# One encoder layer on one core: conditioning parts moved to the first stage, residual loop reordered, affinities kept on chip, experts started on half the rows

## The reference, cut to what matters

```
mod = silu(c) @ w_ada + b_ada          # c: (1024), w_ada: (1024, 6*1024); 6 parts
sh1, sc1, ga1, sh2, sc2, ga2 = split(mod, 6)
h  = rms_norm(x, g_pre1) * (1 + sc1) + sh1
u  = h @ w_in                          # heads' columns, then two gate groups za, zb
y_ret, y_hg = retention(...), hgrn2(...)
merged = sigmoid(za) * (y_ret @ w_br_ret) + sigmoid(zb) * (y_hg @ w_br_hg)
x  = x + ga1 * rms_norm(merged @ w_out, g_post1)
h2 = rms_norm(x, g_pre2) * (1 + sc2) + sh2
aff = softmax(h2 @ w_router); gate, idx = top_k(aff.T, cap)   # 16 experts
x  = x + ga2 * rms_norm(experts(h2[idx]) * gate scattered back, g_post2)
```

## Time and profile before

| what | us |
|---|---|
| median of 3 runs (lowest, highest) | 2854.24 (2853.39, 2854.70) |
| the profiled execution's own time | 2856.68 |
| its span | 2854.7 |
| PE, DVE, ACT, POOL busy | 2665.3, 1786.0, 1335.4, 301.6 |

### The profile page before, as it was taken

One profiled execution on the slowest core, in us unless ns is written; L12 is line 12 of the kernel. 1 busy time (PEld: TensorE's weight loads), 2 busy tenths in 40 slices (PEclk: granted clock), 3 DMA queues, 4 the chain that ended last, 5 costly groups with the idle time before them and its releaser, 6 DMA issues. The chain is left out here.

```text
span 2854.7 us, 48423 instructions
## 1 busy us (share of the span) xinstructions
PE 2665.3 (93%) x20566; PEld 2132.8 (75%) x20566; DVE 1786.0 (63%) x2147; ACT 1335.4 (47%) x1410; POOL 301.6 (11%) x246
## 2 busy tenths in 40 slices
PE   5999999999999988983999999999999999999993
PEld 3788888889877877862777777777777777777772
DVE  4675757767400054547777777776777777777775
ACT  5544435354211121441555555555555555555552
POOL 2010000101000011211011101110111101110110
PEclk9999999999999999995999999999999999999996
DMA  7111011011343265236788788788888888887886
GB/s 283 33 31 44 24 35 55 23 52 31 115 158 126 72 209 166 97 105 242 276 286 298 286 300 289 276 295 291 294 289 296 295 289 284 282 300 286 284 290 230
DMA packets 285775, 564.97 MB, mean 198 GB/s; under 512 B 24680, under 2 KB 91080, under 8 KB 285304
## 3 DMA queue, kind: packets, MB, share of 16 engines
q1 hardware_dynamic: 274536, 540.79, 53.2%
q0 software_dynamic: 7680, 20.98, 3.2%
q10 hardware_dynamic: 3344, 0.11, 0.1%
HBM read 514.52 MB, written 47.28 MB: 197 GB/s over the span
## 5 line engine op out<-in xcount | busy, mean ns | idle before, releaser
L2291 DVE TENSOR_TENSOR we_low<-ring,we_high 128x2048 fp32r<-128x2048 f32 x384 | 878.1, 2291 | 366.5 <-ACT we_high L2240 366.5
L2240 ACT ACTIVATE we_high<-ring 128x2048 fp32r<-128x2048 f32 x384 | 737.4, 1922 | 438.9 <-PE ps_ey L2212 279.7
L1297 PE MATMUL ps_a<-h_high,w_high 128*128 128x512 f32 (+1 forms) x696 | 252.7, 363 | 7.7 <-ACT pair L817 4.8
L1298 PE MATMUL ps_a<-h_low,w_high 128*128 128x512 f32 (+1 forms) x696 | 247.6, 356 | 0.0
L1299 PE MATMUL ps_a<-h_high,w_low 128*128 128x512 f32 (+1 forms) x696 | 247.4, 356 | 0.0
L2179 PE MATMUL ps_ep<-ring,xp 128*32 128x256 f32 x4096 | 234.3, 381 | 0.0
L2210 PE MATMUL ps_ey<-we_high,hidT_high 128*128 128x512 f32 x512 | 206.6, 403 | 0.0
L2154 PE MATMUL ps_eg<-we_high,xs_high 128*128 128x512 f32 x512 | 206.2, 403 | 0.3 <-DVE xs_low L2315 0.3
L2179 PEld LDWEIGHTS ps_ep<-ring,xp 128*32 128x32 f32 x4096 | 126.6, 110 | 99.5 <-issue 22.5
L2156 PE MATMUL ps_eu<-we_high,xs_high 128*128 128x512 f32 x512 | 200.3, 391 | 0.0
L2157 PE MATMUL ps_eu<-we_low,xs_high 128*128 128x512 f32 x512 | 200.2, 391 | 0.0
(11 more groups left out here) (308 smaller groups left out, 4976.3 us busy)
## 6 DMA issues: line engine op xcount, KB each, us to landing
ring<-in_w_gate SPq DMA_DIRECT2D x256, 512.0 KB, 9.4
ring<-in_w_up SPq DMA_DIRECT2D x256, 512.0 KB, 10.5
ring<-in_w_down SPq DMA_DIRECT2D x256, 512.0 KB, 4.4
w_raw<-in_w_in SPq DMA_DIRECT2D x52, 512.0 KB, 3.8
w_ring<-in_w_ada SPq DMA_DIRECT2D x12, 1024.0 KB, 11.1
sig_dram<-sig SPq DMA_DIRECT2D x15, 640.0 KB, 7.1
w_ada_z<-in_w_ada SPq DMA_DIRECT2D x16, 512.0 KB, 6.9
sig_g<-sig_dram SPq DMA_DIRECT2D x16, 512.0 KB, 3.8
```

The lines of the kernel that those rows point to most:

```text
L1297: pe.matmul(out, w_high, x_high, start=start, stop=False)
L1298: pe.matmul(out, w_high, x_low, start=False, stop=False)
L2240: act.activation(w_high[:, s % SPLIT], t.ring[:, s % RAW], ACT.Copy).then_inc(s_high, 1)
L2291: dve.tensor_tensor(w_low[:, s % SPLIT], t.ring[:, s % RAW], w_high[:, s % SPLIT], ALU.subtract).then_inc(s_low, 1)
```

## The change: what it does, and the diff

Parts 3 and 4 of `w_ada` (8 pieces of 1 MiB) and `g_pre2` (1024 numbers as a column) are handled in the first stage, and the gates stage has none of it. The order of the first stage's transfers changes; the squares of the last two pairs of tiles, and their norms, move into the loop over tiles. In the residual stage norms and transposes come one iteration earlier, on ACT and DVE ahead of the newer tile; the last tile's x is added on DVE. The affinities go from SBUF to SBUF at the end of the residual stage. The experts' first products wait for one half of the rows, and PE's `turn_x(0, 2)` comes after the first two pieces.

```diff
-        PARTS = 3
+        PARTS = 5
+            load_w(0)
+            load_w(1)
             load_x(0)
-            load_w(0)
+            load_w(2)
+            load_w(3)
             load_x(1)
-            load_w(1)
+            load_w(4)
             load_x(2)
-            load_w(2)
+            load_w(5)
+            load_head(0)
+            load_w(6)
+            load_w(7)
             load_x(3)
-            load_w(3)
+            load_w(8)
             load_x(4)
-            load_head(0)
-            for j in range(4, NJ):
+            for j in range(9, 4 * PER):
                 load_w(j)
...
             load_head(1)
+            for j in range(4 * PER, NJ):
+                load_w(j)
             load_head(2)
...
                 if i == 0 and v >= 2:
-                    pe.wait_ge(s_modsb, v - 1)
+                    pe.wait_ge(s_modsb, max(v, 2))
...
-                if 2 <= tl < 2 + PER:
-                    mod_rows(COLS1 + tl - 2)
-                if tl in (6, 7):
-                    project(0, KC // 2 * (tl - 6), KC // 2 * (tl - 5))
-            project(1, 0, KC)
+                if tl >= 3:
+                    mod_rows(COLS1 + tl - 3)
+                if tl in (6, 8):
+                    project(0, KC // 4 * (tl - 6), KC // 4 * (tl - 4))
+            mod_rows(4 * PER - 1)
+            project(1, 0, KC // 2)
+            mod_rows(4 * PER)
+            project(1, KC // 2, KC)
+            mod_rows(4 * PER + 1)
             project(2, 0, KC)
+            mod_rows(4 * PER + 2)
+            mod_rows(4 * PER + 3)
+            pe.wait_ge(s_modsb, PARTS)
+            pe.wait_ge(s_xact, NT)
+            pe.wait_ge(s_xdve, NT)
+            columns((3, 4))
...
-                act.dma_start(pre_cols[:], t.g_pre1[0].rearrange("(c p) -> p c", p=P)).then_inc(s_small, 16)
+                for n, v in enumerate((t.g_pre1, t.g_pre2)):
+                    act.dma_start(pre_cols[:, n], v[0].rearrange("(c p) -> p c", p=P)).then_inc(s_small, 16)
...
-            for i in range(NX):
+            for i in range(3):
                 squares(i)
...
+                if tl in (1, 3):
+                    squares(3 + tl // 2)
+                if tl in (3, 5):
+                    root(3 + tl // 4)
...
-                if tl == 8:
+                if tl == 2:
+                    variance(3)
+                if tl == 4:
+                    norm(3)
+                    variance(4)
+                if tl == 6:
+                    norm(4)
+                if tl == 7:
                     rows(2)
                     gate_row(2)
...
+            rows(3)
             low(NT - 1)
+            rows(4)
+            scale_shift(1, t.scale2[:], t.shift2[:])
...
-                    if 3 <= k < 3 + KC and b != 1:
-                        ada(2 * (k - 3) + b // 2)
-                    if k == KC + 4 and b == 0:
-                        columns()
...
-            sp.dma_start(t.aff_dram, affT[:]).then_inc(s["st"], 16)
+            for r, (o, m) in enumerate(((SEQS[0], HALF), (SEQS[0] + HALF, HALF), (0, SEQS[0]))):
+                sp.dma_start(t.shared[r * NE:(r + 1) * NE, 0:m], affT[:, o:o + m]).then_inc(s["st"], 16)
...
-            for k in range(NT + 3):
+            for k in range(NT + 2):
                 if k < NT:
                     out(k)
-                if 2 <= k < NT + 2:
-                    turn(k - 2)
-                if k >= 3:
-                    route(k - 3)
+                if 1 <= k < NT + 1:
+                    turn(k - 1)
+                if k >= 2:
+                    route(k - 2)
...
-            for k in range(NT + 2):
+            for k in range(NT + 1):
+                if k >= 1:
+                    norm(k - 1)
                 if k < NT:
                     act.drain()
                     squares(k)
                 if k + 2 < NT:
                     high(k + 2)
-                if 1 <= k < NT + 1:
-                    norm(k - 1)
-                if k >= 2:
-                    modulate(k - 2)
+                if k >= 1:
+                    modulate(k - 1)
...
+                if tl == NT - 1:
+                    dve.wait_ge(s_x[tl % 3], 16 * (tl // 3 + 1))
+                    dve.wait_ge(s["x1"], tl)
+                    dve.tensor_tensor(x1[:, tl % 3], x1[:, tl % 3], x[:, tl % 3], ALU.add).then_inc(s["x1"], 1)
...
-                if i == 0:
-                    pe.wait_ge(s_xl, 2 * (e + 1))
-                    if b >= 1:
-                        pe.wait_ge(s_hid, b)
+                if i % 2 == 0:
+                    pe.wait_ge(s_xl, 2 * e + i // 2 + 1)
+                if i == 0 and b >= 1:
+                    pe.wait_ge(s_hid, b)
...
-            for r in range(3):
-                turn_x(0, r)
+            turn_x(0, 0)
+            turn_x(0, 1)
             for b in range(NBLK + 1):
                 if b < NBLK:
                     gate_up(b, 0)
                     gate_up(b, 1)
+                if b == 0:
+                    turn_x(0, 2)
```

More of the change, by code:

```diff
@@ L246, in _ @@
             pe.wait_ge(s_modsb, 2)
-            columns()
+            columns((0, 1))
             def project(b, c0, c1):
@@ L304, in _ @@
                     root(i - 1)
-            root(NX - 1)
+            root(2)
             act.wait_ge(s_first, 16)
@@ L338, in rows, with scale_shift @@
                 dve.wait_ge(s_mod, PER * (v + 1))
-                dve.tensor_tensor(mod[:, v], ps_mod[v % 2][:, 0:QW], bias[:, v], ALU.add).then_inc(s_modsb, 1)
-            def scale_shift(scale, shift):
-                dve.wait_ge(s_col, 1)
+                dve.tensor_tensor(mod[:, v], ps_mod[v][:, 0:QW], bias[:, v], ALU.add).then_inc(s_modsb, 1)
+            def scale_shift(n, scale, shift):
+                dve.wait_ge(s_col, n + 1)
                 for r in range(2):
@@ L355, in gate_row, with variance @@
                 dve.tensor_tensor(post[:], mod[:, v], post[:], ALU.mult).then_inc(s_rows, 1)
-            def norm(i):
+            def variance(i):
                 v = ssum[:, 2 * i:2 * i + 2]
@@ L376, in _ @@
             head_columns()
-            for i in range(NX):
+            for i in range(3):
+                variance(i)
                 norm(i)
@@ L1356, in _ @@
                 sp.dma_start(t.yT[:, m], t.yT_dram[m].rearrange("h p n -> p h n")).then_inc(t.s_branch, 16)
-            sp.wait_ge(s_zero, 1)
-            for r in range(2):
-                sp.dma_start(bias[r:P:32], t.b_ada[0][3 * D:5 * D].rearrange("(v g x) -> g v x", g=4, x=QW)).then_inc(s_vec, 16)
-            with nc.allow_non_contiguous_dma(reason="a vector into columns, once"):
-                sp.dma_start(pre_cols[:], t.g_pre2[0].rearrange("(c p) -> p c", p=P)).then_inc(s_vec, 16)
-            load_a(0)
-            load_a(1)
-            for s in t.head_sems:
-                sp.sem_clear(s)
             for k in range(1, NG):
@@ L1659, in _ @@
             pool.memset(zero[:], 0.0).then_inc(s["zero"], 1)
-            for tl in range(NT):
+            for tl in range(NT - 1):
                 pool.wait_ge(s["scaled"], tl + 1)
@@ L1830, in _ @@
             split(1)
-            for k in range(NT + 3):
+            for k in range(NT + 2):
+                if 1 <= k < NT + 1:
+                    variance(1, k - 1)
                 if k < NT:
@@ L1837, in _ @@
                 if 1 <= k < NT + 1:
-                    variance(1, k - 1)
-                if 2 <= k < NT + 2:
-                    modulate(k - 2)
-                if k >= 3:
-                    logits(k - 3)
+                    modulate(k - 1)
+                if k >= 2:
+                    logits(k - 2)
             dve.wait_ge(s["lt"], 1)
```

114 lines of the change are left out of this document (24 added, 90 removed).

## The result

| | before | changed |
|---|---|---|
| median us (lowest, highest) | 2853.53 (2850.98, 2857.42), 8 runs | 2863.1 (2861.89, 2864.38), 8 runs |
| span of the profiled execution | 2854.7 | 2861.1 |

The ratio is 1.0033, 95% interval [1.0024, 1.0042]: 9.6 us slower by the medians. The forecast was 2862.8 (2850 to 2869). The total fits, with luck: the step (a) of the first stage failed, and the terms of the gates stage and of the first stage were each too large by about 3 us or more, with opposite signs.

What follows compares the result with a forecast made beforehand. PE was taken as busy nearly throughout, so what counts is when it gets its work. The terms -17.2 + 22.5 + 1.3 - 0.7 + 2.7 sum to +8.6, giving 2862.8 us on the median's scale, range 2850 to 2869.

Steps and rivals of the forecast that it cites:

- gates stage: Steps 3 to 12 lose all work of the two w_ada parts, which nothing hides behind PE: -17.2 us.
- residual stage: Idle at the start 1.5, one more turn and route +2.9, tail -3.3, slow clock +0.4: about +1.3 us.
- (a): First stage: g_pre2's 1024 small packets cost 8.5 us (bounds 0 and 10.1), so DVE starts at 33.2 instead of 24.7.
- experts' start: First product earlier, but low(2) is late behind x_rows(0, 2), PE idles 3.3 us and its clock falls: +2.7 us.
- two waits for a transfer with the clock that they cost: Gates stage: part of the 17.2 us excess, 3.6 in step 5 (18.99 against 15.36) and another 0.85.
- third rival: The small packets fit in, costing about 1 us: first stage +15, total +1.1, 2855.3 us; chance 0.16.
- (b): First stage, DVE's start to first evacuation: at 51.5, 4.1 us later than now; the earlier weights bring nothing.
- (c): First stage, loop over tiles: piece 12 waits 3.8 us for rows(2), and the stage ends at 102.7 against 79.5.
- fourth rival: PE at the slow clock through the first stage: +30.5 there, total +16.6, 2870.8 us; chance 0.14.
- Transfers alone: Rival: only transfers set the first stage, ending at 82.5, so +3; total -10.9, 2843.3 us; chance 0.12.
- Half rows pay: Rival: if low(2) isn't late, the experts' start gains 2.9 us; total +3.0, 2857.2 us; chance 0.13.
- Slow clock: Rival: first stage near its upper bound from PE's gaps, +30.5; total +16.6, 2870.8 us; chance 0.14.

Runs made afterwards that it cites:

- f_silu_first: Changed kernel with ScalarE's c_silu and c_pad computed ahead of its issues for gn, bias and post: 2867.39 us, ratio 1.0048.
- e_small_alone: Kernel before with only g_pre2's column load added to ScalarE's queue behind g_pre1's (loaded, not used): 2860.68 us, ratio 1.0024.
- g_rows_early: a_low_first with VectorE's rows(2) and gate_row(2) moved ahead of tile 7's evacuation in the first stage: 2849.93 us, ratio 0.9985.
- b_experts_before: Changed kernel with the experts' start put back (three transposes first, both halves of the rows awaited): 2860.33 us, ratio 1.0021.
- a_low_first: Changed kernel with VectorE's low(2) and low(3) ahead of x_rows(0, 2) at the experts' start: 2857.3 us, ratio 1.0009.
- j_norm_early: g_rows_early with ScalarE's root(3) ahead of squares(4) and VectorE's norm(3) behind tile 3 instead of tile 4: 2851.3 us, ratio 0.9987.
- k_all: j_norm_early plus g_pre2's column issued late by SyncE, and the residual stage's old order with last addition on VectorE: 2847.93 us, ratio 0.9979.

## Why the prediction was right

The total was right by luck in part: two errors of opposite sign, each of some 3 us or more, cancel. Step by step, with what the runs put in its place:

| step | predicted | traces of the pair | other runs |
|---|---|---|---|
| gates stage | -17.2 | -17.6 | -13.1 to -14.1 |
| first stage | +22.5 | +19.8 | +17.4 to +19.5 |
| residual stage | +1.3 | +1.8 | +1.4 |
| affinities | -0.7 | -0.35 | -0.1 to -0.4 |
| experts' start | +2.7 | +3.4 | +3.4 by the ratios, +2.6 by the trace |

The first stage of the other runs: 99.26, 99.52 and 99.80 with the parts moved, 80.29 and 81.88 without. Taken back one at a time, the parts give 5.1 (both stages of the move), 3.4 and 2.3 us by the ratios; with the affinities that is 10.4 where 9.6 was measured, each of these figures being good to 3 us or so.

**Gates stage.** The mechanism holds, and the size holds for the two traces. The term "two waits for a transfer with the clock that they cost" (3.6 and 0.85) is the one that was mis-sized: they belong to one execution and not to the kernel. The profiled execution was 2.4 above the median in the table; I took these 2.4 off the sum instead of asking which term they sat in. The 17.2 already took the waits away, so part of the excess was taken off twice. On the median's scale the move gives 13.1 to 14.1 here, and with my other terms as they were the forecast would have been 2865.9 to 2866.9. That it came out within 0.3 us of the measured time is luck: the first stage's term was too large by about as much.

**First stage, (a).** This step failed as an account of the changed kernel: "DVE then starts at 33.2", and it starts at 24.8. Its price was real (6.75 alone, 7.4 in f_silu_first), but I priced the added load against the stream of before. The change rewrote that stream too: in SyncE's new order the fifth piece has to wait for PE by 6.3 us, and PE waited for ScalarE, whose issues the added packets held up. I had the rule that every queue a load stands in counts, and did not apply it to ScalarE's own instructions behind its issues. What I named as the third rival ("the small packets fit in") is what the trace shows, by another mechanism than its own. That equal counts speak against blocks of 9 to 17 was said too soon (e_small_alone, above).

**(b).** With (a) gone, the first evacuation is set by the weights and rows(1) (44.20); "the earlier weights bring nothing" was wrong by 3.2 us.

**(c).** The loop was predicted in the right places (3.8 us at piece 12, measured 3.79) but 4.4 us too short: from the transposes of tile 6 to the end 33.0 against 37.4. The difference is mostly PE at the slow clock behind its gaps (granted 0.57 from 60 to 68 us, so mostly at 1.2 of 2.4 GHz), which I had put into the upper bound and the fourth rival. That bound itself was summed too low: 7 pieces, 4 turns and 4 half blocks at 1.0, 1.0 and 2.75 us are 22 us of work, so at half speed they would add 22 and not 8. In sum the chain was 8.4 earlier than forecast at lb_diff and 7.4 at tile 6's transposes, and lost 4.4 of that behind them: 3.0 earlier than my walk's end of 102.7, 2.7 less than the term of 22.5. g_rows_early shows that the wait at piece 12 with its clock was worth 5.1 in the stage.

**Residual stage.** Its terms (1.5, 2.9, -3.3, 0.4) add up to 1.5 and not 1.3, and the steps to the norm to 12.3 and not 12.7. The two stalls (0.98 and 0.33; 1.0 and 0.5 predicted) and the idle 5.7 are as predicted. From the first to the last squares it is 3.8 more (4.4 predicted), and the tail gives back 2.0 (2.9 predicted), so the size is right with two small errors. Order and last addition together were taken back for 1.4. Of the last addition I had taken for granted that shorter is earlier; in the old order it is not.

**Affinities.** Three issues take 1.89 and not 1.2, and what follows them takes 2.7 and not 3.0, so half of the forecast's gain is left in this trace and less in two others.

**Experts' start.** Right in its mechanism, with the wait at 3.31 where 3.3 was forecast; b_experts_before and a_low_first confirm it from both sides.

**The rivals.** "Transfers alone" falls: piece 12 does wait for DVE, and g_rows_early still ends at 94. (PE's work behind the last tile's turn, put at 16.2 against it, is 16.6 by the walk's own times.) "Slow clock" was half there. "Half rows pay" was a statement on an order that the change did not have; in every trace with that order the stretch is shorter than before.

## What to carry to other kernels

When work is moved onto an engine with a fixed program, look for the instruction that another engine waits for, and where it stands in the order: moving rows(2) up by one tile, and low(2) and low(3) ahead of x_rows(0, 2), turned a kernel that was 0.33% slower into one 0.15% faster. Price an added transfer against the streams of the changed kernel, not of the old one, and count the computations that stand behind a blocked issue. When one of ten equal steps is longer than its neighbours, the excess is that execution's until a second trace shows it. The same holds for a stage that takes a us or two more or less.

## What the runs showed of the hardware that was not expected

- Issuing is not free where many small packets are queued: with 3344 packets in ScalarE's queue over the run one of its issues stood for 4.2 us, with 4400 two stood for 4.8 and 5.3, and the computation behind them came 7.0 us later (11.84; 18.83).
- 1024 packets of 4 bytes cost 6.75 us beside a full stream of 4 KB packets; where the stream ran low, 745 small ones passed in 2 us.
- Short waits on PE cost more than their length when the granted clock falls behind them: 3.3 us of waiting at the experts' start were worth about 5 of the 6.4 gained (the rest is a clock that rose earlier ahead of it), and 3.8 at piece 12 were worth 5.1 in its stage. It does not always fall: behind a wait of 2.71 us tile 8's turn took 1.97 us (j_norm_early), behind one of 2.68 us 1.09 (k_all). And taking 3 us out of a third gap moved piece 12 by 2.0 us and the stage's end by 0.4.
